# Gates of a mixture-of-experts layer: one-hot matmuls, or merged choices and scattered stores

## The chip, the cores and the metric

The kernel runs on one core of one Trainium2 chip. The time is device microseconds of one execution, median of three: 2932.75 us (2931.68 to 2933.92). Views of the profile are of one further execution.

## The reference, cut to what matters

Two transformer blocks on 512 tokens of 1024 values, float32. The first block ends with a layer of 16384 experts. Each of 8 heads of a token scores two sets of 128 keys, takes the best 16 of each half, the best 16 of their sums, and a softmax over these gives the gates:

```
top_s, top_i = lax.top_k(s, 16)
cand = top_s[:, :, 0, :, None] + top_s[:, :, 1, None, :]
best_s, best_c = lax.top_k(cand.reshape(T, 8, 256), 16)
gates = softmax(best_s)
act = gelu(einsum('td,thkd->thk', x, u[expert_idx]))
out = einsum('thk,thkd->td', gates * act, v[expert_idx])
```

A token so has 128 choices. An expert is a pair (first key, second key); several heads of one token may choose the same expert, and their gates then add.

## The kernel before, in words

Tokens stand in 4 blocks of 128. For blocks 0 to 2 (384 tokens) the expert layer is computed densely, for block 3 by gathering its chosen rows.

**First layer.** 128 tiles of weights `u` (one per first key, 128 x 1024). Each float32 tile is split into a high and a low part in a format that TensorE multiplies quickly, and takes 8 x 3 matmuls of 512 columns (`three`, L691 to L693) into bank 0 or 1. GpSimd splits the tiles (`split`, L558 and L560) into two slots. ScalarE applies gelu (L1653) and stores the result to `acts` in DRAM (L1655).

**Choices.** In the same time VectorE chooses for each block (`choose_halves`, `choose`, `places`, `pick_keys`, `picked`, `chosen_gates`, L2307 to L2399). ScalarE does the exponentials (`shares`).

**Dense gates.** For blocks 0 to 2 the gates are laid out as a table over all experts. TensorE transposes the choices (`turn`, L981). For four tokens at a time VectorE compares them with the numbers 0 to 127, which gives one-hot matrices `hot1`, `hot2` (L2437, L2439), GpSimd multiplies by the gates (L574), and TensorE multiplies the two one-hots of each token, 8 matmuls of 256 columns per step of 8 tokens (`gate_batches`, L991). ScalarE and VectorE add the halves into `gate_stage` (L1664, L2449), and ScalarE's queue stores 4 MB per 64 tokens to `gates` (L1676). There are 48 steps; between two stand one or two tiles (`LOT_TILES`).

**Second layer.** 64 units of two keys. SyncE's queue loads activations and gates of each key (L500, L501) and two tiles of `v` (L508). VectorE multiplies activation and gate (`weigh_key`, L2507), ScalarE and VectorE split the product (L1696, L2514) and the tiles (L1691, L2520) into four slots, and TensorE adds all up, 48 matmuls of 384 columns per unit.

**Row sums of block 3.** Beside that GpSimd fetches, by indirect transfers, the activation of each choice (L615) and the row of `v` (L607), and VectorE adds the weighted rows (L2528 to L2535). `sums_of_unit` says in which unit which choice is added: from unit 2 to 61.

Each engine works through its own list in order. SyncE's list also holds the loads of all weights, four tiles ahead of their split (`load`, L453), and 128 copies that set `values` in DRAM (L473), up to the 12th of the 16 tiles of query weights that come before the first layer.

Of the kernel before, what the change touches and what calls it, by code (L numbers as in the profile page):

```python
# [39 lines left out]
LEAD_TILES, TURN_AT = 12, 10  # L40
LONG, TURNING = (2, 2, 2, 1, 2, 2, 2, 2), (2, 2, 2, 1, 2, 2, 1, 2)
LOT_TILES = (LONG, TURNING, LONG, TURNING, LONG, LONG)
TOKENS_PER_BATCH = 4
HOTS = 2
STAGED_TOKENS = 64
LOTS = P // STAGED_TOKENS
LOT_BATCHES = STAGED_TOKENS // TOKENS_PER_BATCH
STEPS = LOT_BATCHES // HOTS
# [3 lines left out]
COPY_FROM = 8  # L52
PAIR_SLOTS = 4
# [95 lines left out]
def build(nc, x, weights, vectors, tables, keys, lru_gates, out):  # L149
# [80 lines left out]
    hot1 = place("hot1", [P, HOTS, TOKENS_PER_BATCH, 2, NKEYS], A0 + 56 * KB, F32R)  # L230
    peer_q = place("peer_q", [P, 16, T], A0 + 64 * KB)
    stage = place("gate_stage", [P, NKEYS, STAGED_TOKENS], A0 + 64 * KB)
# [12 lines left out]
    gates_t = place("gates_t", [P, P], S1 + 7 * KB + 64)  # L245
    hot2 = place("hot2", [P, HOTS, TOKENS_PER_BATCH, NKEYS], S1 + 8 * KB + 64, F32R)
    gate_part = place("gate_part", [P, HOTS, TOKENS_PER_BATCH, NKEYS], S1 + 12 * KB + 64)
# [3 lines left out]
    expert_w = place("expert_w", [P, KEY_SLOTS, DT], A0 + 8 * KB)  # L251
# [4 lines left out]
    v_hi = place("v_hi", [P, 2, 1024], A0 + 40 * KB, F32R)  # L256
    v_lo = place("v_lo", [P, 2, 1024], A0 + 48 * KB, F32R)
    summed = place("token_sums", [P, 1024], A0 + 4 * KB)
    late_slots = [place(f"v_rows{4 + n}", [P, 1024], at * KB) for n, at in enumerate((48, 52, 56, 60))]
    row_slot = [place(f"v_rows{n}", [P, 1024], A0 + at * KB) for n, at in enumerate((16, 20, 56, 60))] + late_slots  # L260
# [45 lines left out]
    gate_sums = [pair[:].rearrange("p b (t part k) -> p (b t) part k", part=2, k=NKEYS) for pair in (df_banks, banks45)]  # L306


    gates = nc.dram_tensor("gates", (DB * LOTS, NKEYS, NKEYS, STAGED_TOKENS), F32, kind="Internal").ap()
# [3 lines left out]
    def sem(name):  # L313
# [27 lines left out]
    ret_s_done, ret_o_done, score_done, turned, batch_done, lru_gate_done = (sem(n) for n in (  # L341
        "ret_s_done", "ret_o_done", "score_done", "turned", "batch_done", "lru_gate_done"))
# [10 lines left out]
    score_read, best_exp, gate_read, ew_hi_ready, lam_by_act = (sem(n) for n in (  # L353
        "score_read", "best_exp", "gate_read", "ew_hi_ready", "lam_by_act"))
# [22 lines left out]
    rot_ready, ret_att, normed, gated, chosen_done, best_shifted = (sem(n) for n in (  # L377
        "rot_ready", "ret_att", "normed", "gated", "chosen_done", "best_shifted"))
    hot_ready, weighted, ew_ready, x_added, lam_by_dve = (sem(n) for n in (
        "hot_ready", "weighted", "ew_ready", "x_added", "lam_by_dve"))  # L380
# [65 lines left out]
    def _(sp):  # L446
# [48 lines left out]
        def load_unit(g, i, u, first):  # L495

            sp.wait_ge(weighted, c.due(weighted, 2, back=2 * AHEAD))
            for e in range(2):
                key, slot = i * (2 * AHEAD) + (g * GROUP + 2 * u + e), 2 * u + e
                sp.dma_start(act_in[:, slot, :], acts[bass.ds(key, 1), :, 0:DT].rearrange("a p n -> (a p) n")).then_inc(key_in[u], 16)  # L500
                sp.dma_start(g_in[:, slot, :].rearrange("p (b t) -> p b t", t=STAGED_TOKENS),  # L501
                             gates[:, :, bass.ds(key, 1), :].rearrange("b k a t -> k b (a t)")).then_inc(key_in[u], 16)
# [7 lines left out]
        sp.wait_ge(gates_out, c.due(gates_out, 16 * DB * LOTS))  # L510
# [36 lines left out]
    def _(pool):  # L547
# [21 lines left out]
        def gate_batch(step, p):  # L569

            pool.wait_ge(hot_ready, c.due(hot_ready, 3))
            first = (step % (LOTS * STEPS) * HOTS + p) * TOKENS_PER_BATCH
            gate = gates_t[:, first:first + TOKENS_PER_BATCH]
            nc.gpsimd.tensor_tensor(hot1[:, p, :, 0, :], f32(hot1[:, p, :, 0, :]),  # L574
                                    gate.unsqueeze(2).to_broadcast((P, TOKENS_PER_BATCH, NKEYS)), ALU.mult).then_inc(hot_gated, 1)

        tile = START["experts"]

        def splits(n):
            for k in range(n):  # L580
                split((tile + k) % RAW)

        splits(LEAD_TILES)
        tile += LEAD_TILES
        for p in range(HOTS):
            gate_batch(0, p)
        ahead = 0
        for step in range(DB * LOTS * STEPS):
            n = LOT_TILES[step // STEPS][step % STEPS]
            n, ahead = n - ahead + (n == 1), int(n == 1)  # L590
            splits(n)
            tile += n
# [1359 lines left out]
    def _(dve):  # L1952
# [439 lines left out]
        def chosen_gates(tt):  # L2392
# [9 lines left out]
            if tt == DB:  # L2402
                return
# [549 lines left out]
```

## Time and profile before

| | |
|---|---|
| median of three | 2932.75 us |
| profiled execution | 2932.43 us |
| its span, first to last instruction | 2930.6 us |
| TensorE busy | 2870.9 us (98%) |
| VectorE, ScalarE, GpSimd busy | 1801.6, 812.7, 2006.7 us |
| granted TensorE clock, mean | 0.993 |
| DMA packets, MB | 269838, 514.79 |

Busy time of TensorE is not time at its peak, since matmuls overlap: a matmul of 512 columns is listed with 390 ns, and the next starts 0.226 us after it. The page's 40 slices are 73.3 us each. The first expert layer lies from 989 to 1735 us, the second from there to about 2277.

### The profile page before, as it was taken

To read this page: it belongs to the slowest core of one execution; us is meant where nothing else is said; L and a number is where in the kernel's file an instruction comes from. 1 tells how busy PE (TensorE), PEld (TensorE's weight loads), DVE (VectorE), ACT (ScalarE), POOL (GpSimd) and SP (SyncE) were. 2 spreads that over 40 slices of the span, in tenths; PEclk is the share of its full clock that TensorE was granted. 3 is DMA by queue.
4 is the path that set the end of the run, shared out by engine and by line. 5 is a ranking of instruction groups with operands and counts; after the bars stand their busy time and mean duration, and the time that the engine had idled before them with its cause. 6 is when DMAs were issued, how large, how long until landed. Compare 5 with 4: busy or idle time off the path is not lost.

```text
span 2930.6 us, 39887 instructions
## 1 busy us (share of the span) xinstructions
PE 2870.9 (98%) x13614; PEld 2415.1 (82%) x13614; DVE 1801.6 (61%) x2935; ACT 812.7 (28%) x1351; POOL 2006.7 (68%) x1095
## 2 busy tenths in 40 slices
PE   7999999999999999999999999999999998999998
PEld 6788877788888888888888879999999765778886
DVE  5578664322125678898884028888887767776611
ACT  3244323321011212212221123333333455322201
POOL 6843574477777688999988776565652651678876
PEclk9999999999999999999999999999999998999999
DMA  4533453355664345545555479999996210223322
GB/s 162 185 117 101 142 167 115 115 190 197 216 201 158 101 138 189 187 151 171 188 191 191 146 241 387 361 352 344 358 357 222 86 62 16 76 88 98 95 93 72
DMA packets 269838, 514.79 MB, mean 176 GB/s; under 512 B 120992, under 2 KB 137504, under 8 KB 268704
## 3 DMA queue, kind: packets, MB, share of 16 engines
q1 hardware_dynamic: 226608, 382.02, 40.0%
q0 software_dynamic: 22528, 67.19, 5.9%
q10 hardware_dynamic: 20592, 64.23, 5.7%
q8 instruction: 54, 0.88, 0.1%
q14 instruction: 56, 0.46, 0.0%
HBM read 452.55 MB, written 127.93 MB: 198 GB/s over the span
## 4 chain that ended last, share of the span: by engine, by line
PE 91%; DVE 4%; POOL 1%; issue 1%; ACT 1%; DMA 1%; POOLq 0%; SPq 0%; ACTq 0%; DVEq 0%
PE bank L691 21%; PE bank L693 20%; PE bank L692 20%; PE banks L691 5%; PE banks L692 5%; PE banks L693 5%; PE banks L842 2%; PE banks L991 2%; PE banks L804 1%; PE banks L806 1%; PE banks L805 1%; PE banks L907 1%; PE bank L868 1%; PE banks L898 1%; POOL w_lo L560 1%
## 5 line engine op out<-in xcount | busy, mean ns | idle before, releaser
L558 POOL TENSOR_TENSOR w_hi<-w_raw,ones 128x1024 fp32r<-128x1024 f32 x364 | 696.9, 1915 | 673.1 <-PE bank L693 438.0
L560 POOL TENSOR_TENSOR w_lo<-w_raw,w_hi 128x1024 fp32r<-128x1024 f32 x364 | 893.6, 2455 | 28.6
L691 PE MATMUL bank<-h_hi,w_hi 128*128 128x512 f32 x2000 | 792.5, 396 | 8.1 <-DVE h_lo L2003 7.0
L693 PE MATMUL bank<-h_hi,w_lo 128*128 128x512 f32 x2000 | 780.1, 390 | 0.0
L692 PE MATMUL bank<-h_lo,w_hi 128*128 128x512 f32 x2000 | 779.2, 390 | 0.0
L691 PEld LDWEIGHTS bank<-h_hi,w_hi 128*128 128x128 f32 x2000 | 376.1, 188 | 92.1 <-DVE h_lo L2003 13.9
L693 PEld LDWEIGHTS bank<-h_hi,w_lo 128*128 128x128 f32 x2000 | 375.6, 188 | 79.9
L692 PEld LDWEIGHTS bank<-h_lo,w_hi 128*128 128x128 f32 x2000 | 376.2, 188 | 74.8 <-issue 2.2
L607 POOL DMA_INDIRECT v_rows<-values,v_row_of_choice x128 | 150.1, 1173 | 147.1 <-DVE token_sums L2535 116.6
L1653 ACT ACTIVATE act_out_stage<-bank 128x512 f32<-128x512 f32 x128 | 76.6, 598 | 578.4 <-PE bank L693 511.7
L615 POOL DMA_INDIRECT row_acts<-acts,act_of_choice x128 | 151.5, 1183 | 46.5 <-issue 38.7
L2535 DVE SCALAR_TENSOR_TENSOR token_sums<-v_rows,row_weights,token_sums 128x1024 f32<-128x1024 f32 x127 | 162.8, 1282 | 0.5
L2507 DVE TENSOR_TENSOR expert_w<-acts_in,gates_in 128x384 f32<-128x384 f32 x128 | 68.8, 578 | 142.8 <-DMA gates_in<-gates 142.8
L2437 DVE TENSOR_TENSOR hot<-bank,tab 128x512 fp32r<-128x512 f32 x192 | 123.3, 684 | 50.5 <-PE banks L991 49.8
L1696 ACT ACTIVATE ew_hi<-expert_w 128x384 fp32r<-128x384 f32 x128 | 60.2, 516 | 192.5 <-PE bank L693 183.8
L2514 DVE TENSOR_TENSOR ew_lo<-expert_w,ew_hi 128x384 fp32r<-128x384 f32 x128 | 67.2, 564 | 72.7 <-ACT ew_hi L1696 72.2
L2449 DVE TENSOR_TENSOR gate_stage<-banks,gate_part 128x512 f32<-128x512 f32 x96 | 97.2, 1093 | 17.9 <-DMA gates<-gate_stage 16.1
L574 POOL TENSOR_TENSOR hot<-hot,gates_t 128x512 fp32r<-128x512 f32 x96 | 98.0, 1041 | 5.8 <-DVE hot L2439 2.0
L691 PE MATMUL bank<-ew_hi,v_hi 128*128 128x384 f32 x256 | 86.3, 337 | 6.8 <-DVE ew_lo L2514 6.7
L693 PE MATMUL bank<-ew_hi,w_lo 128*128 128x384 f32 x256 | 86.8, 339 | 0.0
L692 PE MATMUL banks<-ew_lo,w_hi 128*128 128x384 f32 x256 | 86.7, 339 | 0.0
L691 PE MATMUL bank<-ew_hi,w_hi 128*128 128x384 f32 x256 | 86.7, 339 | 0.0
(480 smaller groups left out, 5581.7 us busy)
## 6 DMA issues: line engine op xcount, KB each, us to landing
w_raw<-weights SPq DMA_DIRECT2D x430, 512.0 KB, 3.6
values<-weights SPq DMA_DIRECT2D x128, 512.0 KB, 4.8
acts<-act_out_stage ACTq DMA_DIRECT2D x128, 256.0 KB, 2.9
v_raw<-weights SPq DMA_DIRECT2D x64, 512.0 KB, 6.5
gates<-gate_stage ACTq DMA_DIRECT2D x6, 4096.0 KB, 13.0
acts_in<-acts SPq DMA_DIRECT2D x128, 192.0 KB
gates_in<-gates SPq DMA_DIRECT2D x128, 192.0 KB
resid<-x SPq DMA_DIRECT2D x4, 512.0 KB, 7.7
```

The source lines that it names most:

```text
L558: nc.gpsimd.tensor_tensor(w_hi[:, pair, :], w_raw[:, slot, :], one_col.to_broadcast((P, 1024)), ALU.mult).then_inc(hi_split, 1)
L560: nc.gpsimd.tensor_tensor(w_lo[:, pair, :], w_raw[:, slot, :], f32(w_hi[:, pair, :]), ALU.subtract).then_inc(split_done, 1)
L574: nc.gpsimd.tensor_tensor(hot1[:, p, :, 0, :], f32(hot1[:, p, :, 0, :]), gate.unsqueeze(2).to_broadcast((P, TOKENS_PER_BATCH, NKEYS)), ALU ...
L607: pool.indirect_dma_start(out=row_slot[j % ROW_SLOTS][:], out_offset=None, in_=value_rows, in_offset=bass.IndirectOffsetOnAxis(ap=v_row[:, ...
L615: pool.indirect_dma_start(out=row_act[:, j:j + 1], out_offset=None, in_=act_words, in_offset=bass.IndirectOffsetOnAxis(ap=act_row[:, j:j + ...
L691: mm(out_, hi, rhs_hi, start=first, stop=False)
L692: mm(out_, hi, rhs_lo, start=False, stop=False)
L693: return mm(out_, lo, rhs_hi, start=False, stop=last)
L1653: fn(act_out_s[:, p, :], bank[p][:], ACT.Gelu_apprx_tanh).then_inc(acc_read_act, 1)
L2437: tt_(hot, tokens[key], t_("iota128").unsqueeze(1).to_broadcast(big), ALU.is_equal).then_inc(hot_ready, 1)
L2449: tt_(stage[:, :, first:first + TOKENS_PER_BATCH].rearrange("p k t -> p t k"), gate_sums[p][:, :, 1, :], gate_part[:, p], ALU.add).then_in ...
L2535: stt(summed[:], rows[:], row_w[:, j:j + 1], summed[:], ALU.mult, ALU.add).then_inc(row_summed, 1)
```

## The change

The table `gates` is now laid out as (first key, second key, token) for 384 tokens. It is filled with zeros by 8 stores from a zero row, in SyncE's list behind the last 8 early loads. The one-hots, their matmuls, the transposes and the stage are gone. VectorE compares a block's 128 choices with each other, multiplies by the gates and sums, so that each choice holds the sum over all choices of the same expert (`merge_equal`, 8 parts of 16 choices); equal choices then hold equal sums. GpSimd writes them one choice at a time, 128 tokens each, with an indirect store into the table; the order does not matter. After 16 stores it waits until they have landed. Since GpSimd no longer splits the first layer's tiles, ScalarE makes their high part and VectorE their low part, into the four slots that the second layer uses. A block's choices are cut into 22 parts, one behind each tile. Row sums run from unit 5 to 62.

```diff
+CHOICE_TILES = 22
+MERGE_PARTS = 8
+SHARES_AT = 7
+HEAD_CHOICES = TOPK
+CLEARS = 8
+FIRST_SUMS = 5
 def sums_of_unit(u):
-    return range(max(u - 2, 0) * CHOICES // (UNITS - 4), min(max(u - 1, 0) * CHOICES // (UNITS - 4), CHOICES))
+    n = UNITS - 1 - FIRST_SUMS
+    return range(max(u - FIRST_SUMS, 0) * CHOICES // n, min(max(u + 1 - FIRST_SUMS, 0) * CHOICES // n, CHOICES))
...
-    gates = nc.dram_tensor("gates", (DB * LOTS, NKEYS, NKEYS, STAGED_TOKENS), F32, kind="Internal").ap()
+    gates = nc.dram_tensor("gates", (NKEYS, NKEYS, DT), F32, kind="Internal").ap()
...
             if COPY_FROM <= n < COPY_FROM + NKEYS:
                 copy_values()
+            clear = n - (len(early) - CLEARS)
+            if clear == 0:
+                sp.wait_ge(consts_set, 3)
+            if clear >= 0:
+                some = NKEYS // CLEARS
+                sp.dma_start(gates[clear * some:clear * some + some, :, :].rearrange("e k t -> k e t"),
+                             zeros[:].unsqueeze(1).to_broadcast((P, some, DT))).then_inc(gates_cleared, 16)
...
-        sp.wait_ge(gates_out, c.due(gates_out, 16 * DB * LOTS))
+        for n in range(DB):
+            sp.wait_ge(gates_added[n], 16 * CHOICES)
...
+        def add_gates(n):
+            pool.wait_ge(rows_ready, n + 1)
+            for j in range(CHOICES):
+                if j and j % HEAD_CHOICES == 0:
+                    pool.wait_ge(gates_added[n], 16 * j)
+                pool.indirect_dma_start(
+                    out=gate_words, out_offset=bass.IndirectOffsetOnAxis(ap=gate_at[:, n, j:j + 1], axis=0),
+                    in_=gate_of[:, n, j:j + 1], in_offset=None).then_inc(gates_added[n], 16)
+        pool.wait_ge(gates_cleared, 16 * CLEARS)
+        for n in range(DB):
+            add_gates(n)
...
+        def tile_hi(n):
+            at = START["experts"] + n
+            act.wait_ge(raw_loaded[n % RAW], 16 * (at // RAW + 1))
+            act.wait_ge(tile_done, at - RAW + 1)
+            fn(value_slot(n)[0], w_raw[:, n % RAW, :], ACT.Copy).then_inc(v_hi_ready, 1)
...
+        for key in range(NKEYS - 2):
+            if key + 3 < NKEYS:
+                tile_hi(key + 3)
+            key_act(key, key % 2)
+            if key % CHOICE_TILES == SHARES_AT and key // CHOICE_TILES < TT:
+                shares()
...
+        def merge_equal(tt, part):
+            n = CHOICES // MERGE_PARTS
+            big, own = (P, n, CHOICES), slice(part * n, part * n + n)
+            pairs = pick[:].rearrange("p a b -> p (a b)").rearrange("p (j k) -> p j k", k=CHOICES)
+            tt_(pairs, chosen[:, 2, own].unsqueeze(2).to_broadcast(big), chosen[:, 2, :].unsqueeze(1).to_broadcast(big), ALU.is_equal).then_inc(dve_step, 1)
+            dve.wait_ge(dve_step, c.due(dve_step))
+            tt_(pairs, pairs, chosen[:, 3, :].unsqueeze(1).to_broadcast(big), ALU.mult).then_inc(dve_step, 1)
+            dve.wait_ge(dve_step, c.due(dve_step))
+            done = rows_ready if part == MERGE_PARTS - 1 else dve_step
+            ve.tensor_reduce(gate_of[:, tt, own], pairs, AX.X, ALU.add).then_inc(done, 1)
...
+        def tile_lo(n):
+            hi, lo = value_slot(n)
+            dve.wait_ge(v_hi_ready, n + 1)
+            tt_(lo, w_raw[:, n % RAW, :], f32(hi), ALU.subtract).then_inc(split_done, 1)
+        def choices(tt, part):
+            if part in (0, 1, 3, 4):
+                choose_halves(tt, *{0: (0, 5), 1: (5, 9), 3: (9, 14), 4: (14, 16)}[part])
+            elif part == 5:
+                choose(0, PEER_HEADS // 2)
+            elif part == 6:
+                choose(PEER_HEADS // 2)
+            elif part == 8:
+                places(tt)
+            elif part == 9:
+                pick_keys(tt, 0)
+            elif part == 10:
+                picked(0)
+                pick_keys(tt, 1)
+            elif part == 12:
+                picked(1)
+                chosen_gates(tt)
+            elif part == 13:
+                place_rows(tt)
+            elif part > 13 and tt < DB:
+                merge_equal(tt, part - 14)
+        for n in range(2, NKEYS):
+            tile_lo(n)
+            if n - 2 < TT * CHOICE_TILES:
+                choices((n - 2) // CHOICE_TILES, (n - 2) % CHOICE_TILES)
```

SyncE's list at the last tiles of the query weights, before: loads (`w_raw`), and copies of `values` up to the 12th tile.

```order
L453 DMA w_raw<-weights 128x1024
L473 DMA values<-weights 128x2x512
L453 DMA w_raw<-weights 128x1024
L473 DMA values<-weights 128x2x512
L453 DMA w_raw<-weights 128x1024 x8
```

The same place now.

```order
L450 DMA w_raw<-weights 128x1024
L470 DMA values<-weights 128x2x512
L489 DMA gates<-zeros 128x16x384
L450 DMA w_raw<-weights 128x1024
L470 DMA values<-weights 128x2x512
L489 DMA gates<-zeros 128x16x384
L450 DMA w_raw<-weights 128x1024
L489 DMA gates<-zeros 128x16x384
L450 DMA w_raw<-weights 128x1024
L489 DMA gates<-zeros 128x16x384
L450 DMA w_raw<-weights 128x1024
L489 DMA gates<-zeros 128x16x384
```

A clear of 16 first keys (`gates<-zeros`) stands behind each of the last eight loads, and with that ahead of the next load.

VectorE's list in the first layer before, one step of 8 tokens with no part of the choices: `hot_115` and `hot_100` are the one-hots of the two keys.

```order
L2437 TENSOR_TENSOR hot_115<-bank,tab 128x512
L2437 TENSOR_TENSOR hot_100<-bank,tab 128x4x128
L2439 TENSOR_TENSOR hot_100<-hot_100,bank 128x4x128
L2437 TENSOR_TENSOR hot_115<-bank,tab 128x512
L2437 TENSOR_TENSOR hot_100<-bank,tab 128x4x128
L2439 TENSOR_TENSOR hot_100<-hot_100,bank 128x4x128
L2449 TENSOR_TENSOR gate_stage<-banks,gate_part 128x4x128 x2
```

VectorE's list now, where the merges of a block begin: `w_lo` or `v_lo` is the low part of a tile, `pick` the table of comparisons.

```order
L2369 CAST gate_row_of_choice<-low_f 128x128
L2392 TENSOR_TENSOR v_lo<-w_raw,v_hi 128x1024
L2377 TENSOR_TENSOR pick<-chosen 128x2048
L2379 TENSOR_TENSOR pick<-pick,chosen 128x2048
L2382 TENSOR_REDUCE gate_of_choice<-pick 128x16
L2392 TENSOR_TENSOR v_lo<-w_raw,v_hi 128x1024
```

Between the low parts of two tiles stand three operations over 2048 elements, in 8 tiles of each of three blocks. The one-hots have gone.

TensorE's list in the first layer before, where the 8 one-hot matmuls (`L991`) stand between two tiles.

```order
L691 MATMUL bank<-h_hi,w_hi 128x512
L692 MATMUL bank<-h_lo,w_hi 128x512
L693 MATMUL bank<-h_hi,w_lo 128x512
L991 MATMUL banks<-hot_100,hot_115 128x256 x8
L691 MATMUL bank<-h_hi,w_hi 128x512
L692 MATMUL bank<-h_lo,w_hi 128x512
L693 MATMUL bank<-h_hi,w_lo 128x512
```

Now the matmuls of two tiles follow each other there.

## Rows read from the trace of the kernel before

**Rows 1.** The page, chain that ended last, by engine

```profile
PE 91%; DVE 4%; POOL 1%; issue 1%; ACT 1%; DMA 1%; POOLq 0%; SPq 0%; ACTq 0%; DVEq 0%
```

**Rows 2.** Sums by stretch: us, PE, PEld, DVE, ACT, POOL, clock, DMA share, GB/s

```profile
1580.00:1735.00 155.00, 155.00 (x685) 128.44 (x685) 9.68 (x8) 19.59 (x32) 122.84 (x59) 1.00 0.53 172
1780.00:2270.00 490.00, 490.00 (x2808) 490.00 (x2807) 403.92 (x485) 172.84 (x234) 267.08 (x227) 1.00 0.96 339
```

**Rows 3.** First layer's first tile (timeline); a one-hot step, the last matmul (chain)

```profile
989.21 0.48 PE L691 MATMUL bank<-h_hi,w_hi 128*128 128x512 f32 x1
...
1055.28 0.94 PE banks L991 x8
...
1735.01 0.25 PE bank L693
```

**Rows 4.** Groups by line: ScalarE's high part, VectorE's low part in the second layer

```profile
L1691 ACT ACTIVATE w_hi<-w_raw 128x1024 fp32r<-128x1024 f32 x32 | 33.8, 1055 | 36.4 <-PE banks L693 35.9 <-ACT act_out_stage L1653 0.5
...
L2520 DVE TENSOR_TENSOR w_lo<-v_raw,w_hi 128x1024 fp32r<-128x1024 f32 x32 | 39.2, 1224 | 6.0 <-ACT w_hi L1691 5.1
```

**Rows 5.** VectorE in order of time, choices of block 0: start, us, line, operation

```profile
980.94 3.19 DVE L2307 MAX8 top_s<-scores 128x8 f32<-128x128 f32 x16 [50.65 <-ACT scores L1642]
...
1000.66 5.00 DVE L2345 TENSOR_TENSOR cand<-top_s 128x512 f32<-128x512 f32 x2
...
1017.21 1.80 DVE L2368 CAST low_f<-best_u 128x128 f32<-128x128 uint32 x1
...
1019.18 2.50 DVE L2371 TENSOR_TENSOR place_f<-place_f 128x256 f32<-128x256 f32 x1
...
1022.64 2.29 DVE L2382 TENSOR_TENSOR pick<-bank,tab 128x2048 f32<-128x2048 f32 x1
1024.97 2.29 DVE L2385 TENSOR_TENSOR pick<-pick,bank 128x2048 f32<-128x2048 f32 x1
...
1037.13 0.59 DVE L2399 TENSOR_TENSOR chosen<-best_s,denom 128x128 f32<-128x128 f32 x1
```

**Rows 6.** ScalarE and its queue in order of time; landing of L1655; page, queue kinds

```profile
1574.81 0.34 ACTq L1676 DMA_DIRECT2D gates<-gate_stage  x1
...
1578.14 0.34 ACTq L1655 DMA_DIRECT2D acts<-act_out_stage  x1
...
1589.65 0.60 ACT L1653 ACTIVATE act_out_stage<-bank 128x512 f32<-128x512 f32 x1 [6.09 <-DMA acts<-act_out_stage]
...
DMA to landing us min/median/max: 2.0/2.9/13.8
...
q10 hardware_dynamic: 20592, 64.23, 5.7%
```

**Rows 7.** Sums by stretch, query weights, one load per tile and no copies

```profile
950.00:960.00 10.00, 10.00 (x46) 8.29 (x45) 0.00 (x0) 1.20 (x2) 7.62 (x5) 1.00 0.33 105
```

**Rows 8.** GpSimd's entries (page, timeline) and VectorE beside them, second layer

```profile
L615 POOL DMA_INDIRECT row_acts<-acts,act_of_choice x128 | 151.5, 1183 | 46.5 <-issue 38.7
...
1819.15 0.94 POOL L615 DMA_INDIRECT row_acts<-acts,act_of_choice  x1 [0.30 <-issue]
1822.01 1.64 POOL L615 DMA_INDIRECT row_acts<-acts,act_of_choice  x1 [0.30 <-issue]
...
1821.60 1.22 DVE L2520 TENSOR_TENSOR v_lo<-v_raw,v_hi 128x1024 fp32r<-128x1024 f32 x1 [0.26 <-ACT v_hi L1691]
1822.75 1.02 DVE L2507 TENSOR_TENSOR expert_w<-acts_in,gates_in 128x384 f32<-128x384 f32 x2
```

**Rows 9.** Between the layers: SyncE's queue, VectorE, chain of waits, TensorE

```profile
1708.61 0.43 SPq L501 DMA_DIRECT2D gates_in<-gates  x1
...
1714.55 4.08 DVE L2507 TENSOR_TENSOR expert_w<-acts_in,gates_in 128x384 f32<-128x384 f32 x2 [139.77 <-DMA gates_in<-gates]
...
1752.16 5.34 DMA row_acts<-acts,act_of_choice
...
1759.11 0.69 PE L691 MATMUL bank<-ew_hi,v_hi 128*128 128x384 f32 x1 [6.65 <-DVE ew_lo L2514]
```

More of the change, by code:

```diff
@@ L567, in _ @@
         c.repeat(START["experts"] // RAW, four)
[L569 to L592, printed above, removed]
-            for p in range(HOTS if step + 1 < DB * LOTS * STEPS else 0):
-                gate_batch(step + 1, p)
-        tail = START["experts"] + NKEYS - tile
-        splits(tail)
-        tile += tail
-        assert tile % RAW == 0
+        gate_words = gates.rearrange("e k (t one) -> (e k t) one", one=1)
+        def add_gates(n):
[9 more added lines that the diff above has]
+            add_gates(n)
         value_rows = values.rearrange("e p half n -> (e p) (half n)")
@@ L666, in _ @@
         c.repeat((N_STREAM - START["up"]) // RAW, four)
-        splits((N_STREAM - START["up"]) % RAW)
+        for s in range((N_STREAM - START["up"]) % RAW):
+            split(s)
         for j in range(0, KT, 2):
@@ L975, in _ @@
         pe.wait_ge(score_read, c.due(score_read, 0, back=4))
-        def turn(tt):
-            pe.wait_ge(chosen_done, c.due(chosen_done))
-            for n in range(4):
-                ins = nc.tensor.transpose(bank[6 + tt % 2][:, n * P:n * P + P], chosen[:, n, :], t_("identity"))
-            ins.then_inc(turned, 1)
-        def gate_batches():
-            for p in range(HOTS):
-                pe.wait_ge(hot_gated, c.due(hot_gated))
-                pe.wait_ge(gate_read, c.due(gate_read, 1, back=HOTS))
-                for t in range(TOKENS_PER_BATCH):
-                    of = (t % 2) * 2 * NKEYS
-                    ins = mm(bank[2 + 2 * p + t // 2][:, of:of + 2 * NKEYS], hot2[:, p, t, :], hot1[:, p, t].rearrange("p a k -> p (a k)"),
-                             start=t % 2 == 0, stop=t % 2 == 1)
-                ins.then_inc(batch_done, 1)
@@ L995, in _ @@
-        tiles_fm(TURN_AT, h_hi, h_lo, acc_read_act)
-        pe.wait_ge(score_read, c.due(score_read, 0))
-        turn(0)
-        tiles_fm(LEAD_TILES - TURN_AT, h_hi, h_lo, acc_read_act)
-        def mixed(n, first, next_choices=0):
-            gate_batches()
-            for k in range(n):
-                p = (first + k) % 2
-                pe.wait_ge(acc_read_act, c.due(acc_read_act, 1, back=2))
-                tile_fm(p, h_hi, h_lo, bank[p][:])
-                if k == 0 and next_choices:
-                    turn(next_choices)
@@ L1007, in twos @@
-        def twos(n, first):
-            c.repeat(n, lambda i: mixed(2, first))
-        tile = LEAD_TILES
-        for lot in range(DB * LOTS):
-            first = tile % 2
-            twos(3, first)
-            mixed(1, first)
-            if LOT_TILES[lot] == TURNING:
-                twos(2, 1 - first)
-                mixed(1, 1 - first, (lot + 1) // LOTS)
-                mixed(2, first)
-            else:
-                twos(4, 1 - first)
-            tile += sum(LOT_TILES[lot])
-        tiles_fm(NKEYS - tile, h_hi, h_lo, acc_read_act)
@@ L1022, in _, with first_layer @@
-        pe.wait_ge(gate_read, c.due(gate_read, 0))
+        def first_layer(i):
+            for n in range(RAW):
+                hi, lo = value_slot(n)
+                pe.wait_ge(acc_read_act, c.due(acc_read_act, 1, back=2))
+                pe.wait_ge(split_done, c.due(split_done))
+                for k in range(KT):
+                    col = slice(k * P, (k + 1) * P)
+                    ins = three(bank[n % 2][:], hi[:, col], lo[:, col], h_hi[:, k, :], h_lo[:, k, :], k == 0, k == KT - 1)
+                ins.then_inc(tile_done, 1)
@@ L1638, in _ @@
         evac(8, peer_q, first=8)
+        def tile_hi(n):
[3 more added lines that the diff above has]
+            fn(value_slot(n)[0], w_raw[:, n % RAW, :], ACT.Copy).then_inc(v_hi_ready, 1)
+        for n in range(2):
+            tile_hi(n)
         for tt in range(TT):
@@ L2420, in place_rows @@
             dve.wait_ge(dve_step, c.due(dve_step))
[L2421 removed]
+            ts(low_f[:], low_f[:], float(DT if tt < DB else T), tiny[:, 44:45], ALU.mult, ALU.add).then_inc(dve_step, 1)
             dve.wait_ge(dve_step, c.due(dve_step))
[L2423 to L2440 removed]
```

196 lines of the change are left out of this document (52 added, 144 removed).

## The prediction

> **What bounds the kernel now.** I read the chain of waits first: TensorE holds 91% of it [rows 1]. So the question is what the change takes from TensorE's queue, and which engine or transfer becomes late in its place. Then the sums by stretch: in the expert layers TensorE is busy without a gap, 685 matmuls in 155.00 us of the first and 2808 in 490.00 us of the second [rows 2]. That is 0.226 us a matmul, and 24 x 0.226 = 5.43 us for one first-layer tile. The first layer runs from 989.2 to 1735.1, 745.9 us [rows 3]; 128 tiles are 695 us of it, and 51 us are something else. Last I read the three engines off the path (VectorE, GpSimd, the transfer queues), since the change moves everything onto them.
>
> **TensorE: -51 us.** Each of 48 steps has 8 one-hot matmuls, 0.94 us together [rows 3]: 45 us. The transposes and the joints around them are the rest. No other work hides them, so all of it goes: -51 us, if the tiles come in time.
>
> **VectorE: +40 us.** The split of a first-layer tile leaves GpSimd. ScalarE makes the high part (1.05 us, on an engine that idles most of the time) and VectorE the low part, 1.22 us [rows 4]; the next operation starts after 1.15 when nothing holds it [rows 8]. Between two tiles VectorE now does one part of the choices. For one block of 128 tokens the parts ran alone from 980.94 to 1037.7: 56.8 us [rows 5]. Three operations in it stood behind GpSimd's splits (5.00, 1.80 and 2.50 us where their sizes want 1.3, 0.3 and 0.4 by their neighbours), so 49.5 us, and some 1.5 us for the places: 51 us. With 14 low parts, 16 us, the first 14 tiles of a block need 67 us of VectorE against 14 x 5.43 = 76 us of TensorE: room. The next 8 tiles carry the merge of equal choices, each three operations of 2048 elements. The same size takes 2.29 us now, spaced 2.33 [rows 5]: 3 x 2.33 + 1.15 = 8.1 us a tile against 5.43. Eight such tiles are 21.4 us too long. There are four split slots, so VectorE can lead: a low part can be ready when tile n-4 is done plus 3.1 us (activation and its queue entry, copy, subtraction), which is 3 x 5.43 - 3.1 = 13.2 us ahead. Block 0 loses 21.4 - 13.2 = 8 us. Block 1 starts without a lead: its first parts (five of the 16 rows that take 19.4 us, and 0.4, with a low part 7.5 us) cost about 4 us, it regains a lead of 11, and the merges cost 21.4 - 11 = 10: 14 us. Block 2 likewise, block 3 only 4 us as it has no merges. Sum 8 + 14 + 14 + 4 = 40 us. Were VectorE's operations 5% quicker this would be 30; 5% slower, 50.
>
> **Clearing the table: +27 us.** SP now sends 8 clears of 3.1 MB (128 x 16 x 384 floats) between the last 8 loads of the query weights. One queue keeps its order: the 256 KB store of activations that ScalarE issued at 1578.14, behind the 4 MB gate store of 1574.81, landed only at 1589.65, after 11.5 us, where 2.9 is its median [rows 6]. Loads on SP's queue at that time were not held up. So each load waits for the clear ahead of it. What a clear costs: ScalarE's queue moved 64.23 MB in 5.7% of 16 engines' span, that is 0.057 x 2930.6 = 167 us, 385 GB/s; 3.146 MB at that rate is 8.2 us. Its runs are 1.5 KB long rather than the 2 KB and 32 KB of that queue, so I take 9. A load is about 1.7 us of all engines (the share was 0.33 over a time with one load per 5.43 us, [rows 7]), a copy of values about 1.2. The first four clears stand with a load and a copy: 11.9 us per tile against 5.43. The next four, 10.7. Over eight tiles that is 90 us of transfers against 43. A load has a slack of 13.5 us (it is issued four tiles ahead, wanted at the split one tile ahead, and takes 3.6), and its landing adds 2 to 4. So 90 - 43 - 13.5 - a few for the copies' place = 27 to 30, and I take +27. From both sides: 14 (a clear of 7.5 us) to 45 (11 us and a dearer copy). Nothing is gained by it anywhere. The Trainium skill (DMA: Bandwidth & Descriptors, section Queues, rings and completion order) says that descriptors on one ring are consumed in order; rows 6 show the same.
>
> **The scatter: +30 us.** 3 x 128 indirect stores of one word per partition, from GpSimd, with a wait for landing after each 16. The table is read when all have landed. GpSimd spends 0.94 us and 0.30 between two when VectorE is quiet, but 1.18 in the mean [rows 8]: an entry that begins while VectorE works on two SBUF operands lasts until that operation ends plus 0.8 us (issued 1822.01, done 1823.65; the subtraction of 1821.60 ended 1822.82). VectorE's own subtraction is no longer for it: 1.22 there, 1.22 in the mean. In merges VectorE holds two operands 5.8 of 8.1 us, in pieces of 2.3 us. So 1.7 us per entry there (bounds 1.44, the present mean with its gap, and 2.03, four entries per tile), and 1.31 elsewhere. A wait costs the landing after the last entry, about 2.6 to 3 us with the activations' stores as the nearest (2.0, 2.9 and 13.8 us at least, median and most, [rows 6]), and 0.75 to restart rather than 0.30: 3.4 us. The first block's choices are merged at tile 24, 137 us after the layer's start at 0. By 473 us (block 3 chosen) come 202 us at 24.4 per 16 entries, 132 of them, and 130 us at 30.6 per 16, 68. The last 184 cost 184 x 1.31 + 11 x 3.4 = 278 us: 751, and 754 landed. The layer ends at 695 + 40 = 735. The first second-layer tile needs the gates 11.5 us before it is to start: four loads (issue 2, landing 4.4), products, high part, low part and the value's low part, as from 1708.6 (queue entries to 1710.1, products at 1714.6 to 1718.6) now [rows 9]. So the gates are wanted at 724, and TensorE waits 30 us. Bounds: none (1.25 per entry, landing in 2), and 80 (2.03 in merges, landing in 4 to 5). After such a wait the matmuls are slow at first, as after the idle of 6.65 us now, where the first lasts 0.69 us [rows 9] against a mean of 0.34: +2.
>
> **Row sums from unit 5: -9 us.** At 1752 TensorE stops 6.65 us because VectorE, in order, waits in unit 2 for the row activations (entries to 1753, landing 1757.5), and then runs slow at first, 2 us more [rows 9]. Unit 5 is 25 us later, so that wait goes, and nothing stands behind it. The last sums move from unit 61 to 62, still before unit 63 where TensorE wants them; a unit with three sums is 8.6 us of VectorE against 8.4 of TensorE, one in five, with lead to spare: nothing. The gates now lie in 1.5 KB runs rather than 256 bytes, which relieves the transfers of the second layer (share 0.96), but TensorE has no gap there: nothing.
>
> **Sum.** -51 + 40 + 27 + 30 + 2 - 9 = +39 us on the profiled execution's 2932.43 us, which is within 0.4 us of the median 2932.75: 2971 us.
>
> **Rivals.**
> - The scatter ends in time (1.25 us per entry, landing in 2 to 2.5 us). For it: most entries now last 0.94. Against: VectorE is fuller in the merges than in any stretch now. 2971 - 32 = 2939.
> - Faster. The clears hide in the slack before the scores and the scatter is in time: 2932 - 51 + 40 - 9 = 2912. It decides at a clear of about 6 us; rows 6 speak against, as that would be 520 GB/s.
> - The scatter is much later, because a landing of single words takes 5 us or the merges let only four entries through per tile. For it: row activations took 5.34 us [rows 9], though under full transfers. +50: 3021.
> - VectorE waits for GpSimd's entries. By the Trainium skill (SBUF — State Buffer, section SBUF: two separate sides) whoever has the shared port pair keeps it for its whole instruction. As a mechanism here: each of two operations in 24 merge tiles would stand 0.5 us behind an entry, and each of 128 low parts a few tenths, +30 us or so on the first layer, of which the late scatter hides a part: 2985. Rows 8 show VectorE's subtraction at its mean beside such an entry, so the chance is small.
> - The clock falls in the gaps of 2.7 us before merge tiles. VectorE sets the pace there, so it costs next to nothing.
>
> **How the numbers follow.** Forecast 0.40; scatter in time 0.20; faster case 0.14; much later 0.19; port held 0.07. Within 0.2% (6 us, about what can be told from no change) falls a part of the second and third, 0.12. Faster by more: 0.16. Slower: 0.72. The forecast's own range is 2950 to 2995. The range for 8 in 10 reaches down into the second case and up to the fourth: 2922 to 3025.
>
> **What would show it.** No one-hot matmuls. TensorE waiting for the loads near 940 to 975 (no such wait: the clears are free). TensorE waiting for VectorE's low parts in the last tiles of the three blocks, some 2.7 us each. At the layer's end a wait of tens of us for the first low part, behind the gates' loads. GpSimd's entries 1.5 to 2 us while VectorE merges. If the first wait is absent and the last too, the forecast is wrong by its sign.

## The result, and the profile after

The changed kernel takes 2968.51 us (median of 4, 2962.25 to 2970.51) where the kernel before took 2932.66 beside it: 1.012 times as long, 95% interval 1.0107 to 1.0134. The forecast was 2971.0. The profiled execution took 2970.51 us, with a span of 2968.7: 38.1 more than the 2930.6 before.

The span splits at three marks of TensorE's timeline: the first matmul of the expert layers, the last of the first layer, the first of the second.

| us | before | after | difference | forecast |
|---|---|---|---|---|
| start to first expert matmul | 989.2 | 1008.6 | +19.4 | +27 |
| first layer | 746.1 | 741.5 | -4.6 | -11 (-51 + 40) |
| wait between the layers | none | 29.4 | +29.4 | +30 |
| from there to the end | 1195.3 | 1189.2 | -6.1 | -7 (-9 + 2) |
| sum | 2930.6 | 2968.7 | +38.1 | +39 |

The page of after, first the chain's shares by engine, then GpSimd's stores (busy, mean ns of one, idle before them), then the queues of SyncE and ScalarE:

```profile
PE 67%; POOL 16%; DVE 6%; issue 5%; DMA 4%; ACT 1%; SPq 0%; POOLq 0%; ACTq 0%; DVEq 0%
...
L581 POOL DMA_INDIRECT gates<-gate_of_choice,gate_row_of_choice x384 | 443.7, 1155 | 330.3 <-DVE gate_of_choice L2382 162.4
...
q1 hardware_dynamic: 161200, 407.19, 39.6%
q10 hardware_dynamic: 19728, 39.07, 3.5%
```

TensorE had 91% of the chain before [rows 1]; now the chain leaves it for the 384 stores and for what follows them.

**The clears.** SyncE's queue in order of time (start, time to hand over). `L450` is a load of query weights, `L489` a clear:

```profile
925.92 0.84 SPq L489 DMA_DIRECT2D gates<-zeros  x1
926.81 8.67 SPq L450 DMA_DIRECT2D w_raw<-weights  x1
...
936.11 0.85 SPq L489 DMA_DIRECT2D gates<-zeros  x1
937.00 8.23 SPq L450 DMA_DIRECT2D w_raw<-weights  x1
```

Each load behind one of the later clears takes over 8 us to be handed over, where it took 0.34 ahead of them. Below stands TensorE, in brackets its idle time and what ended it; then its waits from 900 to 1000 us (sum, times, longest); then the rate over 890:1060 in 40 slices:

```profile
958.93 0.80 PE L680 MATMUL bank<-h_hi,w_hi 128*128 128x512 f32 x1 [4.60 <-POOL w_lo L564]
...
1008.58 0.48 PE L680 MATMUL bank<-h_hi,v_hi 128*128 128x512 f32 x1
```

```profile
PE bank L680 <- POOL w_lo L564: 12.8, 5, 4.6
```

```profile
GB/s 209 188 100 247 160 349 395 407 401 409 402 404 406 401 408 402 408 399 408 402 406 401 404 421 113 197 52 4 0 185 18 167 187 183 85 115 176 150 96 247
```

The transfers run at about 403 GB/s for 75 us. A clear of 3.146 MB is then 7.8 us; I had taken 9. The first expert matmul stood at 989.21 before [rows 3]. Of the 19.4 us, 12.8 are these waits; the rest lies in slow matmuls and restarts behind them (granted clock 0.89 in 950:970 and 0.86 in 970:990).

**The first layer.** VectorE in a merge tile, TensorE behind it, and TensorE's waits of the layer and its end:

```profile
1265.87 2.28 DVE L2377 TENSOR_TENSOR pick<-chosen 128x2048 f32<-128x2048 f32 x1
1268.19 2.29 DVE L2379 TENSOR_TENSOR pick<-pick,chosen 128x2048 f32<-128x2048 f32 x1
1270.51 2.29 DVE L2382 TENSOR_REDUCE gate_of_choice<-pick 128x16 f32<-128x2048 f32 x1
1272.84 1.23 DVE L2392 TENSOR_TENSOR v_lo<-w_raw,v_hi 128x1024 fp32r<-128x1024 f32 x1
```

```profile
1266.01 0.79 PE L680 MATMUL bank<-h_hi,v_hi 128*128 128x512 f32 x1 [2.38 <-DVE v_lo L2392]
1266.60 0.63 PE L681 MATMUL bank<-h_lo,v_hi 128*128 128x512 f32 x1
...
1269.42 0.40 PE L682 MATMUL bank<-h_hi,v_lo 128*128 128x512 f32 x1
1269.65 0.39 PE L680 MATMUL bank<-h_hi,v_hi 128*128 128x512 f32 x1
...
1274.12 0.50 PE L680 MATMUL bank<-h_hi,v_hi 128*128 128x512 f32 x1 [0.81 <-DVE v_lo L2392]
...
1399.46 0.50 PE L680 MATMUL bank<-h_hi,w_hi 128*128 128x512 f32 x1 [2.27 <-DVE w_lo L2392]
...
1407.64 0.50 PE L680 MATMUL bank<-h_hi,w_hi 128*128 128x512 f32 x1 [2.44 <-DVE w_lo L2392]
```

```profile
PE bank L680 <- DVE v_lo L2446: 29.4, 1, 29.4
PE bank L680 <- DVE w_lo L2392: 12.4, 9, 2.4
PE bank L680 <- DVE v_lo L2392: 9.9, 8, 2.4
```

A merge tile is 8.11 us of VectorE (1264.73 to 1272.84, each low part to the next), as worked out. TensorE waits for VectorE 17 times, from 0.3 to 2.4 us, 22.3 us in all. Behind five of the six longest waits (2.3 to 2.4 us) six to eight of the following matmuls start 0.43 us apart instead of 0.23: TensorE's clock is at 1.2 instead of 2.4 GHz there (granted clock 0.50 from 1266.0 to 1268.8). These slow matmuls cost next to nothing, because VectorE sets the pace: the slow tile of 1266.01 is followed by the next after 8.11 us and a wait of 0.81, the fast tile of 1399.46 after 8.18 us and a wait of 2.44. What the slow matmuls take, the next wait gives back.

**The scatter.** The stores and what they waited for; three of them beside that merge tile; then the path at the end of the layer in order of time (start, duration), with short pieces left out:

```profile
L581 POOL DMA_INDIRECT gates<-gate_of_choice,gate_row_of_choice x384: 953/962/3027, 1148.6 to 1759.2; - x192
...
  DVE gate_of_choice L2382: 162.4, 1
  issue: 120.3, 362
  DMA gates<-gate_of_choice,gate_row_of_choice: 47.5, 21
```

```profile
1267.09 1.90 POOL L581 DMA_INDIRECT gates<-gate_of_choice,gate_row_of_choice  x1 [0.31 <-issue]
1269.29 2.02 POOL L581 DMA_INDIRECT gates<-gate_of_choice,gate_row_of_choice  x1 [0.30 <-issue]
1271.62 0.96 POOL L581 DMA_INDIRECT gates<-gate_of_choice,gate_row_of_choice  x1 [0.30 <-issue]
```

```profile
1759.21 2.16 DMA gates<-gate_of_choice,gate_row_of_choice
...
1763.32 0.58 SPq L511
...
1763.94 9.69 DMA w_raw<-weights
...
1775.12 0.95 ACT v_hi L1635
...
1778.07 1.15 DVE v_lo L2446
...
1779.46 0.66 PE bank L680
```

From the layer's start at 1008.6 the first store is at 140.0 (forecast 137) and the last has landed at 752.8 (754). The layer itself ends at 741.5 (735). From the landing to TensorE it is 18.1 us, where the forecast had 11.5: not the gates but the next weights come last. They stand in SyncE's list behind the wait for the gates, are handed over only at 1763.3, and take 9.69 us beside the loads that start with them, while VectorE's products of activation and gate begin at 1769.7. The granted clock in 1750:1780 is 0.56, the last but two column of

```profile
1750.00:1780.00 30.00, 0.59 (x3) 0.57 (x3) 5.01 (x8) 5.39 (x9) 11.55 (x13) 0.56 0.62 230
```

### The profile page after: what moved, and what is told of

Its sections match the earlier page's. It is cut to its first block, busy times and chain, and to the rows that moved or that the text cites. A ratio compares the mean times of both kernels' runs of the same rounds, so it can differ in the third digit from the quotient of the medians.

```text
span 2968.7 us, 38657 instructions
## 1 busy us (share of the span) xinstructions
PE 2849.4 (96%) x13218; PEld 2375.1 (80%) x13218; DVE 1806.3 (61%) x2758; ACT 896.2 (30%) x1383; POOL 1803.7 (61%) x1127
## 4 chain that ended last, share of the span: by engine, by line
PE 67%; POOL 16%; DVE 6%; issue 5%; DMA 4%; ACT 1%; SPq 0%; POOLq 0%; ACTq 0%; DVEq 0%
POOL gates L581 14%; PE bank L680 13%; PE bank L682 13%; PE bank L681 13%; PE banks L680 5%; PE banks L681 5%; PE banks L682 5%; DMA gates<-gate_of_choice,gate_row_of_choice 2%; DMA w_raw<-weights 2%; PE banks L831 2%; PE banks L793 1%; PE banks L795 1%; PE banks L794 1%; PE banks L896 1%; POOL w_hi L562 1%
## 5 line engine op out<-in xcount | busy, mean ns | idle before, releaser
L562 POOL TENSOR_TENSOR w_hi<-w_raw,ones 128x1024 fp32r<-128x1024 f32 x236 | 454.2, 1924 | 584.7 <-PE bank L682 335.2
L581 POOL DMA_INDIRECT gates<-gate_of_choice,gate_row_of_choice x384 | 443.7, 1155 | 330.3 <-DVE gate_of_choice L2382 162.4
L680 PE MATMUL bank<-h_hi,w_hi 128*128 128x512 f32 x1488 | 597.7, 402 | 33.3 <-POOL w_lo L564 13.8
L564 POOL TENSOR_TENSOR w_lo<-w_raw,w_hi 128x1024 fp32r<-128x1024 f32 x236 | 585.1, 2479 | 18.5
L682 PE MATMUL bank<-h_hi,w_lo 128*128 128x512 f32 x1488 | 583.4, 392 | 0.0
L681 PE MATMUL bank<-h_lo,w_hi 128*128 128x512 f32 x1488 | 582.8, 392 | 0.0
L680 PEld LDWEIGHTS bank<-h_hi,w_hi 128*128 128x128 f32 x1488 | 281.7, 189 | 106.4 <-POOL w_lo L564 17.6
L680 PE MATMUL bank<-h_hi,v_hi 128*128 128x512 f32 x512 | 204.8, 400 | 9.9 <-DVE v_lo L2392 9.9
L681 PE MATMUL bank<-h_lo,v_hi 128*128 128x512 f32 x512 | 203.0, 397 | 0.0
L682 PE MATMUL bank<-h_hi,v_lo 128*128 128x512 f32 x512 | 203.0, 396 | 0.0
L2392 DVE TENSOR_TENSOR w_lo<-w_raw,w_hi 128x1024 fp32r<-128x1024 f32 x64 | 78.5, 1229 | 111.8 <-ACT w_hi L1599 110.8
L681 PEld LDWEIGHTS bank<-h_lo,v_hi 128*128 128x128 f32 x512 | 97.4, 190 | 22.2
```

Source lines behind the costliest of these rows:

```text
L562: nc.gpsimd.tensor_tensor(w_hi[:, pair, :], w_raw[:, slot, :], one_col.to_broadcast((P, 1024)), ALU.mult).then_inc(hi_split, 1)
L564: nc.gpsimd.tensor_tensor(w_lo[:, pair, :], w_raw[:, slot, :], f32(w_hi[:, pair, :]), ALU.subtract).then_inc(split_done, 1)
L581: pool.indirect_dma_start(out=gate_words, out_offset=bass.IndirectOffsetOnAxis(ap=gate_at[:, n, j:j + 1], axis=0), in_=gate_of[:, n, j:j + ...
L680: mm(out_, hi, rhs_hi, start=first, stop=False)
L681: mm(out_, hi, rhs_lo, start=False, stop=False)
L682: return mm(out_, lo, rhs_hi, start=False, stop=last)
```

## The experiments

Theory: four separate causes, as forecast: clears in front of loads, VectorE's merges, a scatter that begins too late, and the row sums. Rivals stand with each run. Twelve kernels ran on four chips, which I sort into two kinds by the time of the kernel before beside them: on one chip (e5 to e8) it took 2932.6 us, as it did when the change was timed, on three others (e1 to e4, e9 and e10, e11 and e12) 2943.6 to 2945.8. The changed kernel took 2968.5 us where it was first timed and 3384.7 on one of the three (e11), so the kinds are told apart throughout: A for 2932.6, B for 2944 to 2946.

### Chips of kind A

**e5, a quarter of each merge**

```diff
+            n //= 4
...
+            if part == 0:
+                ve.tensor_copy(gate_of[:, tt, :], chosen[:, 3, :]).then_inc(dve_step, 1)
```

> The changed kernel with a quarter of each merge: its three operations cover 4 of a part's 16 choices, so three quarters of the merging are left out. The prediction's way of adding up (VectorE's delay of TensorE and the wait for the scatter are separate terms): both clocks and waits of the first layer go, about 40 us less, 2928. Rival (one path: merges of block 0, then 384 stores, then the wait; what TensorE gains in blocks 1 and 2 it gives back waiting for the scatter, which begins only some 5 us earlier): the first layer ends about 40 us sooner and the wait at its end grows by about as much, 5 to 25 us less in all, 2944 to 2963.

The kernel leaves three quarters of the merging out. Measured: 2911.96 us (2910.68 to 2913.72), 56.5 less than the changed kernel, more than either said. TensorE's only wait from the first layer's start to past its end, and the stores:

```profile
PE bank L680 <- DVE v_lo L2450: 8.9, 1, 8.9
```

```profile
L581 POOL DMA_INDIRECT gates<-gate_of_choice,gate_row_of_choice x384: 954/962/2005, 1125.5 to 1703.2; - x192
```

The layer ends 35.7 us sooner (1008.57 to 1714.31, 705.7 us), yet the wait shrinks by 20.5 instead of growing. The stores explain it: they begin 23.1 us earlier, since block 0's merges come first on that path, and take 577.7 instead of 610.6 us, since an entry is long only beside VectorE's large operations (1065 ns in the mean instead of 1155, 34.8 us over 384 entries). 23.1 + 32.9 = 56.0 us, the whole gain. So it is one path, as the rival had it: merges of block 0, 384 stores, loads. Its size was wrong, because the merges lengthen that path twice.

**e6, two stores per block**

```diff
-            sp.wait_ge(gates_added[n], 16 * CHOICES)
+            sp.wait_ge(gates_added[n], 16 * 2)
...
-            for j in range(CHOICES):
+            for j in range(2):
```

> The changed kernel with 2 instead of 128 indirect stores for each block of rows, so that nearly all gates stay zero in the table: merges, clears and reads remain. My theory (the scatter holds up only the end of the first layer): the wait of 29.4 us goes and nothing else, 29 to 31 us less, about 2938. Rival (the stores also delay VectorE's work on the weights in the first layer, by GpSimd's share of the access to the SBUF): 10 or more us below that, under 2930.

The kernel leaves nearly all gates out of the table. Measured: 2939.41 us (10 runs, 2938.16 to 2940.67), 29.1 less than the changed kernel, as the theory had it. The first layer lies from 1008.69 to 1749.7, 741.0 us against 741.5: the stores don't slow VectorE. Its low parts last 1224 ns here and 1229 beside the stores. TensorE's waits:

```profile
PE bank L680 <- DVE v_lo L2392: 11.3, 6, 2.4
PE bank L680 <- DVE w_lo L2392: 10.2, 6, 2.3
```

The Trainium skill (SBUF — State Buffer, section SBUF: two separate sides) has whoever holds the shared port pair keep it for the whole instruction while the other blocks. Here little of that shows in the other direction: entries of 0.96 us become 1.9 to 2.0 beside VectorE, while VectorE's operations stay at 2.28 and 1.23, but for a few low parts of 1.30 (the longest here is 1.23).

**e7, spaced clears and a scatter by parts**

```diff
-            clear = n - (len(early) - CLEARS)
+            clear, odd = divmod(n - (len(early) - 2 * CLEARS), 2)
...
-            if clear >= 0:
+            if clear >= 0 and not odd:
...
-            pool.wait_ge(rows_ready, n + 1)
...
+                if j % (CHOICES // MERGE_PARTS) == 0:
+                    pool.wait_ge(rows_ready, n * MERGE_PARTS + j * MERGE_PARTS // CHOICES + 1)
```

> The changed kernel with both edits: spaced clears and a scatter that follows each part of the merge. My theory (the two waits have nothing in common): their gains add, 48 to 50 us less than the changed kernel, about 2919. Rival (the first layer begins 19 us sooner, so the merges and the stores begin sooner too but the scatter's length is fixed and it is late again at the border): 20 to 30 us less, 2938 to 2948.

Measured: ten runs fall in two groups, three at 2920.8 to 2923.6 and seven at 2930.4 to 2933.8; median 2931.24, ratio to the kernel before 0.999 (0.998 to 1.0). So the median is 37.3 us below the changed kernel and lies between the theory (2919) and the rival (2938 to 2948); neither is borne out by it. The profiled run, 2921.81, is one of the three. In it both causes are gone and the gains add: the first expert matmul is at 990.98, 17.6 us sooner, and the second layer follows the first without a wait.

```profile
990.98 0.48 PE L682 MATMUL bank<-h_hi,v_hi 128*128 128x512 f32 x1
...
1732.95 0.34 PE L682 MATMUL bank<-ew_hi,v_hi 128*128 128x384 f32 x1
```

```profile
L583 POOL DMA_INDIRECT gates<-gate_of_choice,gate_row_of_choice x384: 952/958/3035, 1074.2 to 1706.0; - x192
```

The last store starts at 1706.0 and lands some 2 us later, 25 us before the layer's end, and the loads behind it need up to 18. So some 7 us of cover are left. What takes 10 us in the other seven runs is open, since none of them was profiled; their mean granted clock was 0.990 to 0.991, that of the three 0.992 to 0.993.

**e8, the merge in smaller pieces on top**

```diff
-CHOICE_TILES = 22
-MERGE_PARTS = 8
+CHOICE_TILES = 30
+MERGE_PARTS = 16
...
```

> As the one with both edits, and the merge is cut into 16 parts of 8 choices instead of 8 parts of 16, laid over 30 instead of 22 tiles. My theory (VectorE delays TensorE because three operations of 2.3 us stand between two of its evictions): with operations half as long TensorE's 22 us of waits for VectorE in the first layer and its slow matmuls behind the gaps go, and the sum is 2875 to 2885. Rival (VectorE's work is what is too much in that stretch, however it is cut): no difference from the kernel with both edits, about 2919.

Measured: 2886.91 us (2885.83 to 2888.09), 0.9846 of the kernel before (0.9829 to 0.9862), 2 us above the theory's range. TensorE's only wait from 1000 to 1785, and the layer's ends:

```profile
PE bank L682 <- ACT act_out_stage L1620: 0.2, 1, 0.2
```

```profile
991.57 0.48 PE L682 MATMUL bank<-h_hi,v_hi 128*128 128x512 f32 x1
...
1697.16 0.34 PE L682 MATMUL bank<-ew_hi,v_hi 128*128 128x384 f32 x1
```

The same number of elements is merged, so VectorE had the time; what delayed TensorE was 7 us of merging between two low parts, 8.11 us a tile against TensorE's 5.5, where it is now 3.7 and 4.9. The layer takes 705.6 us, as in e5. Two kernels without a wait in the layer thus give both terms: 741.5 - 705.6 = 35.9 us for VectorE's delay, and 746.1 - 705.6 = 40.5 us for what TensorE saves. Set against e8 tile by tile, the changed kernel loses 11.0 us in block 0, 12.2 in block 1, 12.1 in block 2 and nothing in block 3. This version beats both kernels on kind A; on kind B it did not run.

### Chips of kind B

**e1, only the row sums moved, in the kernel before**

```diff
-    return range(max(u - 2, 0) * CHOICES // (UNITS - 4), min(max(u - 1, 0) * CHOICES // (UNITS - 4), CHOICES))
+    n = UNITS - 1 - 5
+    return range(max(u - 5, 0) * CHOICES // n, min(max(u + 1 - 5, 0) * CHOICES // n, CHOICES))
```

> The kernel before, with one edit: the row sums begin at unit 5 instead of unit 2. My theory (the 6.65 us for which TensorE waited at 1759.11 us end when the row activations' rows need not be there in unit 2, and the slow clock behind that gap goes with it): 7 to 9 us less than the kernel before, about 2925. Rival (VectorE or the row sums fall due later and the wait comes back in unit 5): no difference, 2932.7.

Measured: 2939.07 us against 2943.57 (12 and 17 runs, 2927.07 to 2956.67 and 2933.05 to 2946.63); ratio 0.9995 (0.9975 to 1.0014). The spread is wider than the effect, so the time tells nothing. In the trace the wait of 6.65 us [rows 9] is gone: no wait for another engine from 1730 to 2300 is over 0.5 us. But TensorE has 7.2 us of "issue" there, in 11 waits, and the kernel before on kind A has none. So kind B differs even without the stores, in the stretch where GpSimd fetches the rows of block 3.

**e2 (row sums at unit 2), e3 (spaced clears), e4 (scatter by parts)**, each one edit of the changed kernel. e3 and e4 are the two halves of e7's edit; e2 is

```diff
-    n = UNITS - 1 - FIRST_SUMS
-    return range(max(u - FIRST_SUMS, 0) * CHOICES // n, min(max(u + 1 - FIRST_SUMS, 0) * CHOICES // n, CHOICES))
+    return range(max(u - 2, 0) * CHOICES // (UNITS - 4), min(max(u - 1, 0) * CHOICES // (UNITS - 4), CHOICES))
```

> The changed kernel with the row sums at unit 2, as before the change. My theory: the wait for the row activations comes back, now behind the 384 stores of the gates on GpSimd, and costs what it cost before or more: 7 to 12 us above the changed kernel's 2968.5, 2976 to 2980. Rival (the 29.4 us for which TensorE waits for the scatter cover it already, since the loads of the row activations run in that gap): no difference, 2968.5.

> The changed kernel with its eight clears of the table placed behind every second of the last sixteen early loads instead of behind each of the last eight. My theory (the clears delay the loads that the preparation of the first expert's weights waits for, since all stand in SP's one queue, and spaced twice as wide each fits into that queue's slack): TensorE's waits for the low parts go and the first expert matmul comes back from 1008.6 towards 989 us, so up to 19.4 us less, 2949 to 2955. Rival (the bytes of the clears cost their time wherever they stand in front of the experts): no difference, 2968.5.

> The changed kernel, in which GpSimd waits for each eighth of a block's merge instead of for all of a block, so that its stores begin about 57 us earlier (at about 1092 instead of 1148.6 us). My theory (the 29.4 us at 1779 are the tail of 384 stores in a row, begun too late): the wait goes, 29 to 31 us less, 2938 to 2940. Rival (the wait is one for weights at the border of the layers, or the entries become slower beside the merges): it keeps half or more of its length, 2953 to 2968.

Measured: 3338.4, 3371.1 and 3171.3 us, all far outside what any theory said. None of the three questions is answered by these times. The part of e3 ahead of the stores can be read all the same: its first expert matmul is at 992.83, where e1 on the same chip has 989.50. e2 was not repeated.

**e9 and e10, e3 and e4 once more**

> The kernel with spaced clears once more. On its chip the kernel before took 2943.6 us and all three changed kernels 3171 to 3371, with TensorE idle for nothing that the profile shows (a matmul every 2.8 us) as long as GpSimd's stores ran; on another chip four kernels with the same stores took 2887 to 2939. Theory (that is the chip's, and has nothing to do with the clears): on a chip where the kernel before takes 2932 to 2933, 2949 to 2955, with the first expert matmul at about 990 and the wait for the scatter still there. Rival (the spacing of the clears starts it): 3300 or more again.

> The kernel with the scatter by parts once more, for the same reason. Theory: 2938 to 2941 where the kernel before takes 2932 to 2933, as the 29.4 us of waiting go and the late start of the first layer stays. Rival (the chip has no part in it): 3170 again.

Measured: 3373.8 and 3161.6 us, with the kernel before at 2945.1: a chip of kind B again. In e9 the first expert matmul is at 990.52, in e10, with the clears left as they were, at 1006.96. No store has run by then. So clears that stand twice as far apart cost 1 to 3 us in front of the layer (e3, e7, e9) instead of 17 to 19.

**e11, the changed kernel itself, and e12, the two stores of e6**

> The changed kernel as it is, once more, as a control for the five runs in which TensorE stood idle for nothing that the profile shows while the 384 stores ran. Theory (a chip's property decides, and the kernel before shows which: 2932 on one kind, 2944 on the other): 2968 where the kernel before takes 2932 to 2933, and 3300 to 3400 where it takes 2944. Rival (only the variants do this): 2968 to 2980 on either.

> The changed kernel with 2 instead of 128 stores for each block (most gates stay out of the table), on the same chip as its control. Theory (the one-word stores of GpSimd are what starves TensorE of instructions): 2938 where the kernel before takes 2932 to 2933, and no more than 2960 where it takes 2944. Rival (the clears, the merges or the loads of the changed kernel do it): 3100 or more where the kernel before takes 2944.

Measured: 3384.66 us (3319.0 to 3395.36) and 2956.75 (2955.81 to 2959.19), with the kernel before at 2945.77. So the changed kernel takes 15% longer than the kernel before on such a chip, and neither the spacing of e9 nor the parts of e10 started it. Nearly all of it hangs on the stores: with 6 of them instead of 384 it is 11 us. Sums by stretch of e11 (TensorE, its weight loads, VectorE, ScalarE, GpSimd, each with its count; then clock, share and rate of transfers), then TensorE in it:

```profile
1143.00:1300.00 157.00, 47.09 (x129) 30.62 (x127) 40.33 (x184) 6.62 (x8) 111.06 (x113) 0.60 0.10 31
1300.00:1430.00 130.00, 105.84 (x424) 83.41 (x425) 98.77 (x112) 34.31 (x41) 18.50 (x20) 0.88 0.31 103
```

```profile
1237.39 0.79 PE L680 MATMUL bank<-h_hi,v_hi 128*128 128x512 f32 x1 [19.82 <-issue]
...
1240.54 0.63 PE L681 MATMUL bank<-h_lo,v_hi 128*128 128x512 f32 x1
1241.55 0.39 PE L682 MATMUL bank<-h_hi,v_lo 128*128 128x512 f32 x1 [0.38 <-issue]
1244.34 0.40 PE L680 MATMUL bank<-h_hi,v_hi 128*128 128x512 f32 x1 [2.40 <-issue]
1247.14 0.59 PE L681 MATMUL bank<-h_lo,v_hi 128*128 128x512 f32 x1 [2.41 <-issue]
```

The same first stretch in the changed kernel on the chip where it was first timed, and in e12:

```profile
1143.00:1300.00 157.00, 146.49 (x607) 116.59 (x607) 153.93 (x363) 44.26 (x53) 111.97 (x90) 0.97 0.40 128
```

```profile
1143.00:1300.00 157.00, 144.78 (x609) 115.84 (x608) 153.96 (x360) 44.28 (x54) 5.11 (x4) 0.98 0.38 129
```

While GpSimd stores, TensorE starts eight matmuls at the slow clock's pace and then one every 1.4, 2.1 or 2.8 us, and waits for nothing that the profile shows (316 us of "issue" from 1000 to 1900). Some 6 us after the stores of block 0 and of block 1 end, it runs on. ScalarE is held up too: it reads at 1535.58 a tile whose last matmul began at 1516.65. VectorE as well: 40.33 us busy in the stretch instead of 153.93. The transfers are nearly idle (share 0.10), and GpSimd itself is not slowed (0.96 us an entry). That the stores do it is shown by e12. How they hold the other engines up is not: all of them at once would fit a delivery of instructions that the one-word writes crowd out, but no run tests that.

Not tried: a scatter without the wait after each 16 stores.

## Why the prediction was right

The time was right to 0.1%, and the four places were right: clears, merges, late scatter, row sums. That it came so close is luck in part: TensorE saved 10.5 us less than forecast, while VectorE cost 4.1 and the clears 7.6 less. Of its steps:

- **TensorE -51.** Mis-sized: -40.5 (e8). I took 0.226 us a matmul from [rows 2], and all 685 matmuls there are indeed those of tiles. But over the whole first layer of the kernel before they start 0.2273 us apart within tiles, 698 us for 3072 of them, so products, transposes and joints were 48 us. And in e8, without a wait, they start 0.2297 apart, 5.51 us a tile, which takes 7 us of that back. Why the tiles became slower is open.
- **VectorE +40.** 35.9 (e8, e5). The pace of 8.1 us per merge tile was exact. By block it was 11, 12, 12 and 0 instead of 8, 14, 14 and 4: block 3 costs nothing. The waits, 22.3 us, are less than the delay, since slow matmuls and the restart behind each gap fill the rest. The clock does fall in the gaps, and that it "costs next to nothing" was right: VectorE sets the pace there.
- **Clears +27.** Mis-sized: +19.4. The order within a queue, read from [rows 6], holds on SyncE's too; the rate was 403 GB/s instead of the 350 behind 9 us a clear. 8 x 1.2 = 9.6 us covers the difference of 7.6.
- **Scatter +30.** 29.4, but by two errors that cancel: the layer ended 6.5 us later than forecast, and the way from the landing to TensorE was 6.6 us longer. The step that fails is that TensorE would start 11.5 us after the gates, "four loads (issue 2, landing 4.4), products, high part, low part and the value's low part, as from 1708.6": it left out the weight load queued behind the waiting instruction. In the kernel before the first two of those loads were handed over at 1718.24, 17 us before the layer's end.
- **Row sums -9, slow clock +2.** -6.1 measured as the remainder of the trace; without the wait between the layers the rest of the span is 1186.9 to 1187.2 (e6: 2936.6 - 1749.7, e7, e8), 8.1 to 8.4 less than before. The difference of some 2 us fits slow matmuls behind the wait, as forecast. No run isolates it cleanly (e1 is inconclusive, e2 lost).
- **The sum as such.** It holds, since the wait was worked out against the layer's end. But its terms are not what taking each away would give. In e5 three quarters of the merges were worth 56.5 us, not 40: much of the first layer's 35.9 us lies hidden behind the scatter, and when the second layer starts is set by the path merges of block 0, stores, loads. With the first edit that shortens the scatter, VectorE's delay comes to the surface (e7).
- **The port rival** (VectorE waits for entries) fell: e6.
- On kind B the prediction would have been wrong by 400 us. Nothing in the profile of before, taken on kind A, speaks of it, and no rival had anything like it.

## What to carry to other kernels

Where one queue or engine has to carry a new piece of work, what matters is what stands behind it in order: a clear in front of a load, a weight load behind a wait for gates. Space bulk transfers so that each fits the slack between two loads, cut what an engine has to do per tile to less than the tile takes (4.9 us of VectorE instead of 8.1, against TensorE's 5.5, gained 36 us), and start a long chain of stores as soon as its first input is there. And measure a kernel with hundreds of one-word stores on more than one chip: the same kernel took 2962 us at the least on one chip and 3395 at the most on another.

## What the runs showed of the hardware

- Two kinds of chip: 0.4% apart for a kernel without one-word stores (2932.6 and 2943.6 to 2945.8), 14% with 384 x 128 of them (2968.5 and 3384.7). With the scatter by parts it was 3171 and 3162 (e4, e10).
- An indirect store of one word in each of 128 partitions: 0.96 us and 0.30 to the next; 1.9 to 2.0 beside VectorE's operations of 2048 elements; landed 2.16 us after the start of the last.
- Behind five of six gaps of 2.3 to 2.4 us six to eight of TensorE's next matmuls were 0.43 us apart (granted clock 0.50), behind the sixth they were not. The slow ones cost nothing where VectorE set the pace.
- With 3 MB clears between them, each load took 8.2 to 8.7 us to hand over on SyncE's queue, at 399 to 409 GB/s.
